# The masks of the attention weights, logarithms and ML weights and the product of the ML gates on VectorE, in place of GpSimd, in a one-core encoder layer

## What is computed

```python
# attention, 8 heads of 128, strictly causal (valid: key position < query position)
z = einsum('bqhd,bkhd->bhqk', q, k) * scale
log_1m = where(valid, log_sigmoid(-z), 0.0)                  # the logarithms, masked
after = cumsum(log_1m, axis=3, reverse=True) - log_1m
a = where(valid, exp(log_sigmoid(z) + after), 0.0)           # the weights, masked
sb_y = einsum('bhqk,bkhd->bqhd', a, v)
# mLSTM, 4 heads of 256 (causal: key position <= query position)
w_intra = where(causal, exp(d - m_t), 0.0)                   # the ML weights, masked
s = einsum('bhld,bhsd->bhls', q, k) * w_intra
h = (s @ v + w_inter * q @ c) / max(abs(sum(s) + w_inter * q @ n), exp(-m_t))
ml_y = rmsnorm(h) * hnorm * sigmoid(o)
# merge
merged = sum(sigmoid(gate_i) * ((y_i * silu(z_i)) @ w_branch_i) for i in (pool, sb, ml))
y = x + rmsnorm(merged @ w_out)
```

## Time and profile before

| | |
|---|---|
| median of 3 runs | 2347.35 us (2345.71 to 2348.9) |
| the profiled execution, its own time | 2346.01 us |
| its span, from first to last instruction | 2344.4 us |
| granted TensorE clock, mean of the span | 0.987 |
| busy: PE, DVE, ACT, POOL | 2260.0, 1469.4, 923.5, 243.2 us |
| masks on POOL: XD, XC, W_ml | 24.6, 24.3, 13.0 us |
| product of the gates on POOL, 4 times | 10.6 us |

### The profile page before, as it was taken

How to read it: one execution, slowest core, us unless ns; L and a number is a source line. 1 busy time by engine, 2 the same in 40 slices (tenths; PEclk the granted TensorE clock), 3 DMA queues, 4 the chain that set the end, 5 groups by cost and what they waited for, 6 DMA issues and landing times.

```text
span 2344.4 us, 40436 instructions
## 1 busy us (share of the span) xinstructions
PE 2260.0 (96%) x16616; PEld 2222.1 (95%) x16616; DVE 1469.4 (63%) x1636; ACT 923.5 (39%) x1232; POOL 243.2 (10%) x293
## 2 busy tenths in 40 slices
PE   3799999999999999999999999999899999999996
PEld 3799999999999999999999999999898999999996
DVE  5867686766666666677666666665665677653233
ACT  4334333334433344444444444443554233322221
POOL 3200000000010000111000000000344222000000
PEclk7899999999999999999999999999999999999998
DMA  5234444344444444444344443446556556745222
GB/s 153 60 106 121 125 112 125 105 138 121 129 114 131 113 119 129 119 112 133 109 128 121 121 129 113 118 126 208 189 192 204 185 175 192 192 117 184 77 72 98
DMA packets 415437, 311.29 MB, mean 133 GB/s; under 512 B 11181, under 2 KB 376869, under 8 KB 413296
## 3 DMA queue, kind: packets, MB, share of 16 engines
q1 hardware_dynamic: 396432, 247.76, 38.3%
q0 software_dynamic: 18848, 61.25, 7.4%
HBM read 250.06 MB, written 58.90 MB: 132 GB/s over the span
## 4 chain that ended last, share of the span: by engine, by line
PE 91%; DVE 4%; issue 1%; ACT 1%; POOL 1%; DMA 1%; DVEq 0%; POOLq 0%; ACTq 0%
PE pp L738 64%; PE pp L875 11%; PE pp L1058 9%; PE M L746 1%; PE M L978 1%; PE M L932 1%; PE M L995 1%; PE M L912 1%; PE M L838 1%; PE M L902 1%; PE M L1035 1%; DVE xa L1514 1%; DVE XA L1837 1%; POOL xt L2129 0%; DVE wa_lo L1471 0%
## 5 line engine op out<-in xcount | busy, mean ns | idle before, releaser
L738 PE MATMUL pp<-xa,wa_hi 128*128 128x288 f32 x7680 | 1543.7, 296 | 26.5 <-DVE wa_lo L1471 14.8
L738 PEld LDWEIGHTS pp<-xa,wa_hi 128*128 128x128 f32 x7680 | 1235.6, 188 | 29.0 <-DVE xa L1514 10.8
L738 PE MATMUL pp<-xa,wa_lo 128*128 128x288 f32 x3840 | 1131.6, 295 | 0.0
L738 PEld LDWEIGHTS pp<-xa,wa_lo 128*128 128x128 f32 x3840 | 725.9, 189 | 0.0
L1471 DVE TENSOR_TENSOR wa_lo<-raw_a,wa_hi 128x1024 fp32r<-128x1024 f32 x274 | 340.9, 1247 | 253.5 <-ACT wa_hi L1096 253.4
L1096 ACT ACTIVATE wa_hi<-raw_a 128x1024 fp32r<-128x1024 f32 x274 | 289.1, 1056 | 225.4 <-PE pp L738 218.7
L1471 DVE TENSOR_TENSOR wa_lo<-raw_r,wa_hi 128x1024 fp32r<-128x1024 f32 x136 | 173.2, 1274 | 141.5 <-ACT wa_hi L1096 141.5
L1096 ACT ACTIVATE wa_hi<-raw_r 128x1024 fp32r<-128x1024 f32 x136 | 143.5, 1055 | 133.5 <-PE pp L738 133.5
L875 PE MATMUL pp<-gt_hi,wb_hi 128*128 128x288 f32 x768 | 168.7, 301 | 0.0
L875 PE MATMUL pp<-gt_hi,wb_lo 128*128 128x288 f32 x768 | 164.5, 296 | 0.0
L875 PE MATMUL pp<-gt_lo,wb_hi 128*128 128x288 f32 x768 | 164.2, 295 | 0.0
(11 more groups left out here) (286 smaller groups left out, 2119.9 us busy)
## 6 DMA issues: line engine op xcount, KB each, us to landing
raw_a<-in_w_in_dram SPq DMA_DIRECT2D x206, 512.0 KB, 5.0
raw_r<-in_w_in_dram SPq DMA_DIRECT2D x68, 512.0 KB, 5.0
z_scratch<-zs POOLq DMA_DIRECT2D x60, 576.0 KB, 3.3
raw_b<-in_w_branch_dram SPq DMA_DIRECT2D x48, 512.0 KB, 4.4
raw_b<-in_w_out_dram SPq DMA_DIRECT2D x32, 512.0 KB, 4.1
gz<-z_scratch SPq DMA_DIRECT2D x48, 288.0 KB, 4.4
qkv<-z_scratch SPq DMA_DIRECT2D x23, 288.0 KB, 5.0
gt_hi<-gated_scratch SPq DMA_DIRECT2D x4, 1152.0 KB, 7.3
```

Of the source, the lines that this page charges most:

```text
L738: i = nc.tensor.matmul(out, ws[:, slot, k, :], xa[:, o, part, k, :], start=opens and k == 0 and s == 0, stop=k == HK - 1 and s == 2, skip_ ...
```

## The change

`apply_mask` moves from GpSimd's block to VectorE's, and with it the three masks; the product of the gates moves too. The semaphore `Wm_ready` goes, since VectorE now masks and multiplies `W_ml` itself; a new one, `mask_ready`, tells VectorE that `mask` is built. The places in VectorE's order: the logarithms are masked directly behind `logs(i)`; the weights of head i-2 behind `logits(i)`, in front of a `split_lo`; those of head 6 behind the last `logs_lo`; those of head 7 in front of the last `gate_head`; the ML weights behind the merges and in front of the wait for the scores; the product of the gates behind the merges that follow L1992, in front of L1997. In `build_mask` the last step is no longer a link with a wait of its own but signals `mask_ready`. GpSimd keeps the building of the mask and all its stores.

```diff
@@ -425,7 +425,7 @@
         mrow_loaded, mem_loaded = sem("mrow_loaded"), sem("mem_loaded")
         zg_ready = sem("zg_ready")
         c0_loaded, mktr_done, mkhi_ready, kw_ready = sem("c0_loaded"), sem("mktr_done"), sem("mkhi_ready"), sem("kw_ready")
-        D_ready, W_ready, Wm_ready = sem("D_ready"), sem("W_ready"), sem("Wm_ready")
+        D_ready, W_ready, mask_ready = sem("D_ready"), sem("W_ready"), sem("mask_ready")
         scores_done, sw_ready, mvtr_done, mvtok_ready = sem("scores_done"), sem("sw_ready"), sem("mvtr_done"), sem("mvtok_ready")
         shi_ready, slo_ready, mvhi_ready = sem("shi_ready"), sem("slo_ready"), sem("mvhi_ready")
         num_done, num_ready, squares_ready = sem("num_done"), sem("num_ready"), sem("squares_ready")
@@ -1821,6 +1821,20 @@
                     dve.wait_ge(xclo_ready, i)
                 nc.vector.scalar_tensor_tensor(XC[:, :], XA[i % 2][:, :], 0.0, XB[:, :], ALU.max, ALU.add).then_inc(L_ready, 1)
 
+            def apply_mask(X, masked):
+                for col, c, w in masked:
+                    i = nc.vector.tensor_tensor(X[:, col:col + w], X[:, col:col + w], mask[:, c:c + w], ALU.mult)
+                return i
+
+            def mask_logs(i):
+                dve.wait_ge(mask_ready, 1)
+                dve.wait_ge(L_ready, i + 1)
+                apply_mask(XC, SB_MASKED).then_inc(Lm_ready, 1)
+
+            def mask_weights(i):
+                dve.wait_ge(a_ready, i + 1)
+                apply_mask(XD, SB_MASKED).then_inc(am_ready, 1)
+
             def logs_lo(i):
                 dve.wait_ge(xchi_ready, i + 1)
                 nc.vector.tensor_tensor(XC_lo[:, :], XC[:, :], XC_hi[:, :].bitcast(F32), ALU.subtract).then_inc(xclo_ready, 1)
@@ -1863,11 +1877,13 @@
             merge(0)
             key_tokens(1)
             logs(0)
+            mask_logs(0)
             merge(1)
             logits(1)
             split_lo(At(3))
             logs_lo(0)
             logs(1)
+            mask_logs(1)
             split_lo(At(4))
             value_tokens(0)
             exponents(0)
@@ -1876,15 +1892,18 @@
                 logs_lo(i - 1)
                 merge(2 * i - 2)
                 logits(i)
+                mask_weights(i - 2)
                 split_lo(At(2 * i + 1))
                 merge(2 * i - 1)
                 gate_head(i - 2)
                 logs(i)
+                mask_logs(i)
                 gated_lo(PG + i - 2, zsb[i % 2][:, :])
                 split_lo(At(2 * i + 2))
                 value_tokens(i - 1)
                 exponents(i - 1)
             logs_lo(SBH - 1)
+            mask_weights(SBH - 2)
             split_lo(At(H_SB + 1))
             merge(H_SB - 2)
             gate_head(SBH - 2)
@@ -1892,6 +1911,7 @@
             merge(H_SB - 1)
             value_tokens(SBH - 1)
             exponents(SBH - 1)
+            mask_weights(SBH - 1)
             gate_head(SBH - 1)
             gated_lo_direct(PG + SBH - 1, SBH - 1, zsb[1][:, :])
 
@@ -1945,7 +1965,7 @@
 
             def ml_head(i):
                 h = H_SB + 4 * i
-                steps.begin(0, 3 + MC)
+                steps.begin(0, 4 + MC)
                 decay_rows(i)
                 dve.wait_ge(mkhi_ready, i + 1)
                 if i:
@@ -1960,8 +1980,10 @@
                     merges(i - 1, STATE)
                 split_lo(At(h + 2))
                 merges(i, KTR)
+                dve.wait_ge(mask_ready, 2)
+                dve.wait_ge(W_ready, i + 1)
+                steps.link(apply_mask(W_ml, ML_MASKED))
                 dve.wait_ge(scores_done, i + 1)
-                dve.wait_ge(Wm_ready, i + 1)
                 nc.vector.scalar_tensor_tensor(W_ml[:, :], M[:, 0:ML_W], MDH ** -0.5, W_ml[:, :], ALU.mult, ALU.mult
                                                ).then_inc(sw_ready, 1)
                 if i:
@@ -1992,6 +2014,9 @@
                 nc.vector.scalar_tensor_tensor(den[:, :], den[:, :], DEN_MIN, EM_h[:, :], ALU.max, ALU.max).then_inc(dmax_ready, 1)
                 split_lo(At(h + 5))
                 merges(i, WEIGH)
+                dve.wait_ge(mo_loaded, 16 * (i + 1))
+                dve.wait_ge(mg_loaded, 16 * (i + 1))
+                nc.vector.tensor_tensor(zml[:, :, :], zml[:, :, :], oml[:, :, :], ALU.mult).then_inc(zg_ready, 1)
                 dve.wait_ge(ssq_done, i + 1)
                 dve.wait_ge(dsq_ready, i + 1)
                 nc.vector.scalar_tensor_tensor(two(den[:, :]), M[:, 0:1024].rearrange("p (b t) -> p b t", b=2)[:, :, 0:TH],
@@ -2106,20 +2131,16 @@
             steps.end(1)
 
             def build_mask(strict):
-                steps.begin(0, 1 + len(MASK_KEYS) + 1)
+                steps.begin(0, 1 + len(MASK_KEYS))
                 steps.link(nc.gpsimd.memset(mask[:, :], 1.0))
                 for j, kb in enumerate(MASK_KEYS):
                     c, w = (j * P, P) if kb < NT else (j * P, TS)
                     steps.link(nc.gpsimd.affine_select(mask[:, c:c + w], mask[:, c:c + w], pattern=[[1, w]],
                                                        compare_op=ALU.is_gt if strict else ALU.is_ge, fill=0.0,
                                                        base=0 if kb < NT else TS, channel_multiplier=-1))
-                steps.link(nc.gpsimd.affine_select(mask[:, c:c + w], mask[:, c:c + w], pattern=[[0, w]],
-                                                   compare_op=ALU.is_ge, fill=0.0, base=-TS, channel_multiplier=1))
+                i = nc.gpsimd.affine_select(mask[:, c:c + w], mask[:, c:c + w], pattern=[[0, w]],
+                                            compare_op=ALU.is_ge, fill=0.0, base=-TS, channel_multiplier=1)
                 steps.end(1)
-
-            def apply_mask(X, masked):
-                for col, c, w in masked:
-                    i = nc.gpsimd.tensor_tensor(X[:, col:col + w], X[:, col:col + w], mask[:, c:c + w], ALU.mult)
                 return i
 
             pool.wait_ge(gain_loaded, 16)
@@ -2229,7 +2250,7 @@
                     store_pair(At(LOOP_EV + q, i, 6), "sigmoid")
 
 
-            build_mask(True)
+            build_mask(True).then_inc(mask_ready, 1)
 
             def store_keys(i):
                 pool.wait_ge(ktok_ready, i + 1)
@@ -2250,30 +2271,20 @@
                     pool.dma_start(gated_v[:, s, tile, :], src[:, :]).then_inc(g_stored, 16)
 
             for i in range(SBH + 2):
-                if i >= 2:
-                    pool.wait_ge(a_ready, i - 1)
-                    apply_mask(XD, SB_MASKED).then_inc(am_ready, 1)
                 if i < SBH:
                     store_keys(i)
-                    pool.wait_ge(L_ready, i + 1)
-                    apply_mask(XC, SB_MASKED).then_inc(Lm_ready, 1)
                 if 2 <= i < SB_STORED + 2:
                     store_gated(PG + i - 2, KW + i - 2)
                 if 1 <= i <= SBH:
                     store_values(i - 1)
 
             pool.wait_ge(am_ready, SBH)
-            build_mask(False)
+            build_mask(False).then_inc(mask_ready, 1)
 
             def ml_head(i):
-                pool.wait_ge(W_ready, i + 1)
-                apply_mask(W_ml, ML_MASKED).then_inc(Wm_ready, 1)
                 if i:
                     for c in range(MC):
                         store_gated(PG + SBH + MC * (i - 1) + c, 2 * KW + MC * (i - 1) + c)
-                pool.wait_ge(mo_loaded, 16 * (i + 1))
-                pool.wait_ge(mg_loaded, 16 * (i + 1))
-                nc.gpsimd.tensor_tensor(zml[:, :, :], zml[:, :, :], oml[:, :, :], ALU.mult).then_inc(zg_ready, 1)
                 pool.wait_ge(state_ready, i + 2)
                 own_wait()
                 for s, dst in enumerate((p_c_v, s_c_v)):
```

## The result

The change made the kernel slower: 2353.66 us, median of 8 runs (2351.56 to 2356.53), against 2347.03 us for the kernel before on the same chip (2345.71 to 2348.9, 8 runs). The ratio is 1.0029, 95% interval 1.0019 to 1.004, so 6.8 us, between 4.5 and 9.4. The forecast of no change that can be measured, 2348.9 us within 2345.6 to 2352, is wrong. The profiled execution took 2353.24 us around a span of 2351.6, where the kernel before had 2346.01 and 2344.4.

A forecast was written before the change was run, and what follows sets the result against it. The prediction took TensorE, busy 96% of the span, as the bound; other work counts only where TensorE waits. First heads 0.05, last heads 0.15 and mLSTM head 2 1.27 made +1.5 us on 2347.35: 2348.9 us, range 2345.6 to 2352.

The forecast's parts named there:

- the rival without overlap: Instructions on VectorE don't overlap: a mask group costs 1.23 us, the product 1.35; +2.1 us, 2349.5; chance 0.15.
- The waits in attention: TensorE waits 2.5 us at L932, 3.5 at the third head's keys, 2.2 at head 6's weighing, none at head 7's.
- Behind mLSTM head 2: After L1997 in head 2, TensorE waits 0.7 us at ml_k's transposes, 0.6 at the scores; +1.27 us in all.
- The product with the scores: mLSTM masks: L1965 of heads 1 and 2 comes 0.6 us later, at no cost to TensorE.
- the forecast of 0.2: Masks' cost in attention: +0.05 us in the first heads, +0.15 in the last, nothing in heads 2 to 7.
- The step that failed: Gate product, mLSTM heads 0, 1, 3: L1997 0.8 to 0.9 us later, nothing lost; head 3 reads its states last.
- Sum: +0.05 us, and the wait there grows from 2.53 to 3.5: First attention heads: earlier logarithms cut one wait of TensorE from 3.4 to 2.5 us, handed back at the third head's keys.
- +0.15 us: Last attention heads: head 6's masks end later, +0.5 us; head 7's wait of 0.34 us goes.
- the rival of the sooner store: Head 1's states land sooner, so the 1.3 us wait for mk_lo in mLSTM head 2 goes: +0.2 us, 2347.6; chance 0.15.
- the slower one: Masks take GpSimd's 1.85 us a group, delaying the weighing in six attention heads: +6.5 us, 2354; chance 0.05.
- something that I don't see, mostly slower: Chance of 0.05 kept for an outcome outside the forecast and its rivals, with no place or size given.

The follow-up runs named there:

- product alone: Kernel before with only the product of the ML gates moved to VectorE, in front of L1997; 2350.55 us, ratio 1.0019 to the kernel before.
- product in the gap in heads 0 to 2: Changed kernel, product behind the copies of num and den in mLSTM heads 0 to 2, before L1997 in the last; 2352.22 us, 1.0017 to the kernel before.
- before, second profile: Kernel before, unchanged, profiled once more; one execution, 2348.36 us.
- after, second profile: Changed kernel, unchanged, profiled once more; one execution, 2352.51 us.
- head 1's logarithms masked later: Changed kernel with the mask of head 1's logarithms behind exponents(0) instead of before the fifth block's split; 2351.0 us, 1.0014 to the kernel before.
- head 6's weights masked first: Changed kernel with the mask of head 6's weights in front of logs_lo of head 7; 2351.34 us, 1.0017 to the kernel before.
- the two with the edited stores: n_out stored in front of the last head's states: on the changed kernel 2363.25 us (1.0069), on the kernel before 2348.27 us (1.0004).
- the last two gap runs: Changed kernel, product behind the copies of num and den in the last mLSTM head alone (2348.87 us, 1.0005), or in heads 0 to 2 alone (2352.22, 1.0017).
- the gap's in all heads: Changed kernel with the product behind the copies of num and den in every mLSTM head; 2348.93 us, 1.0007 to the kernel before.
- the delay in the kernel before: Kernel before, masks on GpSimd, plus four idle 128-column products on VectorE behind logs(1); 2350.35 us, 1.0013 to the kernel before.

## Why the prediction was wrong

**What held.** The price of the work: a group of masks 0.96 to 0.97 us (0.98 forecast), the product 1.35, so the rival without overlap is out. (The prediction took only half of the section "The DRAIN you can't avoid" of the Trainium skill, "VectorE: DVE Perf Modes": the section adds that a next instruction that is not held starts earlier. The trace agrees with that: four masks of 0.30 us on average ended 0.96 us after the first start. The four parts, as the prediction prints them, add up to 1.22 and not 1.23 us; nothing hangs on it.) The waits in attention: 2.3, 3.6, 2.2 us and none, where 2.5, 3.5, 2.2 and none were forecast; no wait at the weighings of heads 0 to 5. Behind mLSTM head 2, 0.53 us at the transposes and 0.38 at the scores for 0.7 and 0.6. The product with the scores came 0.6 us later in head 2, as forecast, and 0.1 in head 1, for 0.6. The masks' sum: alone they cost 1.4 us (-0.7 to 3.5), which can't be told from the forecast of 0.2.

**The step that failed, and carries most of the loss.** "In heads 0, 1 and 3 L1997 waited for TensorE for some of the time, so it comes 0.8 to 0.9 us later; [...] and head 3 reads its states last." The delay is right: in all six profiles with the product there in the last head, its states leave GpSimd 0.76 to 0.82 us later relative to TensorE than in the kernel before (in the changed kernel at 2019.10 - 3.98 = 2015.12 us for 2014.31). It was then given the price nothing, because TensorE's transposes of a next head don't wait for the last states. But the store of `n_out`, which GpSimd issues behind them, leaves late too, and ACT's `m_hi`, the weights behind it, the merge and TensorE wait for its landing. Take the start of the first `m_hi` and subtract how late TensorE is in that profile at head 3's scores:

| kernel | m_hi, corrected, us | TensorE's wait at L875, us |
|---|---|---|
| before | 2028.61 | 0 |
| product alone | 2029.52 | 0.36 |
| product in the gap in heads 0 to 2 | 2029.72 | 0.58 |
| before, second profile | 2029.97 | 0.84 |
| after | 2030.65 | 1.50 |
| after, second profile | 2030.96 | 1.80 |
| head 1's logarithms masked later | 2031.98 | 2.83 |
| head 6's weights masked first | 2032.27 | 3.17 |

The wait is the corrected start less 2029.15 us in every row that has one, to 0.06. The kernel before had 0.54 us to spare in its first profile, and none in the second. The 0.8 us use that up, and above it the landing of `n_out` counts in full. The delay alone is not the whole of it: the slower of the two stores took 11.4 to 14.2 us in the six profiles with the product in that place in the last head, 12.7 on average, and 10.6 to 11.8 us, 11.2 on average, in seven of the eight others (the eighth, the second of before, has no record of it; its `m_hi` came 1.4 us later than in the first). Why it lands 1.5 us later there is open. The mean wait over the six profiles of kernels with the product in that place in the last head is 1.7 us, against 0.1 over the eight others, the two with the edited stores left out. The table counts the wait alone: behind the longest, 3.17 us, the clock fell as well, and TensorE lost about 2.7 us more. By the times the whole of the product's place is 5.2 us, the last head's part somewhere in 2.4 to 5.6 (the ratios of the last two gap runs against the changed kernel's and the gap's in all heads: 1.0029 to 1.0005, and 1.0017 to 1.0007). The profiles account for about 2 us in the last head and 1 in head 2 of the 5.2; the remainder of 2 us is inside the intervals, and I can't name it. A single profile can be far from its kernel's median: that of the product alone, with its wait of 0.36 us, is the fastest of 11 runs, 3.1 us under their median.

**The term left out.** "Sum: +0.05 us, and the wait there grows from 2.53 to 3.5", and for the last heads "+0.15 us". Both count only the wait; the prediction has no term for the clock. Behind a wait of 3.6 us or more at the third head's keys the granted clock fell in each of the five profiles that have one (the changed kernel, the three with the product in the gap and attention as in the changed kernel, and the delay in the kernel before), for 1.5 to 2.5 us. Behind 2.5 us it did not, in the kernel before and three others; behind 2.0 us it did once, in the kernel with head 6's weights first, where it had just fallen behind L932. At head 6's weighing it fell behind 2.2 us in six of eight profiles, for 1.5 to 1.7 us, and behind GpSimd's 1.73 us in none of five. At L932 it fell behind 3.4 us in three of four and behind 2.2 to 2.9 in four of twelve: there TensorE has the next wait to make it up, and little of the loss is left. So the same wait ended at either level from one execution to the next, in the kernel before itself at L932. The Trainium skill says in "TensorE: Matmul & The Clock Gate", Part 1, that the watch on the engine's activity runs on its own and is not started by the kernel, and that the number of slow matmuls at a kernel's start differs between runs for that reason. The falls here, in the middle of a kernel, go with it; no run tests the reason. The masks' 1.4 us fit 0.5 + 1.5 at the weighing less 0.5 at head 7, and leave nothing for the third head's keys; how often the fall there costs its 2.5 us in a plain run was not measured.

**What the single profile hid.** The first profile of the kernel before misled in two places: it lacks the late weights at L1058 (1.1 to 1.6 us in the fifteen other profiles), and it has the wait of 1.3 for `mk_lo` in head 2, which was shorter in the changed kernel by 1.1: the rival of the sooner store. But the second profile of the kernel before has it too: most of the wait for mk_lo (1.1 us) is in head 3 there. The two nearly cancel, and neither belongs to the change.

Of the rivals the slower one gave the right size, 2354 us, by a mechanism that did not happen: no group took over 0.97 us. The 0.05 for "something that I don't see, mostly slower" was the place of the truth, and too little for a kernel in which TensorE is busy 96% of the time and every other engine's lateness can turn into a wait.

## What to carry to other kernels

Follow a delayed instruction to everything that waits for it, stores and their landing included, until a reader has room to spare; "the last of its kind" has readers of another kind. Price an idle stretch of TensorE that grows by what comes behind it too, and put moved work where the engine already waits for another: the change as it stands made this kernel 6.8 us slower; the same masks in other places, with the product left on GpSimd, made it 2.3 us faster (0.2 to 4.5). And where an argument goes by waits of 1 us, take a second profile of the kernel before and more of the changed one: two profiles of the kernel before differed by 2.3 us at the end with the same instructions.

## What the hardware showed

The granted clock fell behind waits of as little as 2.2 us in attention, in some executions and not in others, and stayed at 0.50 for 3.4 to 10.2 us. Two stores of 4 KB, in pieces of single numbers, took 9 to 14 us to land, much longer than 256 KB of states (5.8 us) beside them (in the changed kernel with the edit 12 and 21 us); put in front of those, they pushed the states to 19.7 us and the weights to 13.7 in one kernel, and the states to 11.7 and the weights to 4.8 in the other, for the same edit. Why it was so much worse in the changed kernel is open. (The Trainium skill, "DMA: Bandwidth & Descriptors", puts a strided or non-contiguous last dimension at one descriptor per element; long landings for 4 KB go with it, but no run here counts descriptors.) VectorE's products of 128 columns took 1.98 us for four beside GpSimd's mask and 0.96 for a whole group of masks, 576 columns, when GpSimd had none.
